# A hybrid decoder layer: stage seams, the top-k search's steps, and mixing's output projection in three passes

## The reference

```
hn = rms_norm(x, g_pre_mix);  q,k,v,index,deltanet,ssm parts = split(hn @ w_in)
o_a = attention over the 256 best keys of each query (index scores, top-k)
o_b = gated DeltaNet scan;  o_c = Mamba-2 scan            (causal convs + SiLU ahead)
mix = concat(o_a, o_b, o_c) @ w_out;   x = x + rms_norm(mix, g_post_mix)
hn = rms_norm(x, g_pre_x);  x = x + rms_norm(softmax((hn @ w_xq) mem_k) mem_v @ w_xo, g_post_x)
hn = rms_norm(x, g_pre_ffn); gate, up = hn @ w_gate, hn @ w_up
x = x + rms_norm((silu(conv3(gate)) * up) @ w_down, g_post_ffn)
```

## Time and profile before

| | us |
|---|---|
| median of 3 runs | 4142.58 (4139.6 to 4143.28) |
| the profiled execution | 4146.24 |
| its span, first to last instruction | 4144.1 |
| PE busy | 3807.1 (92%) |
| DVE, ACT, POOL busy | 1937.2, 1691.0, 654.3 |
| mean granted clock of PE | 0.943 |

### The profile page before, as it was taken

The page is one execution under the profiler, slowest core; times in us unless marked ns, Lnnn a source line. Parts: engine busy times, 40 slices in busy tenths (PEclk is TensorE's granted clock), DMA queues, the critical chain, the costliest instruction groups (busy, mean ns, idle before and its releaser), DMA issues. The chain is left out here.

```text
span 4144.1 us, 53976 instructions
## 1 busy us (share of the span) xinstructions
PE 3807.1 (92%) x20439; PEld 3243.0 (78%) x20439; DVE 1937.2 (47%) x3066; ACT 1691.0 (41%) x2923; POOL 654.3 (16%) x397
## 2 busy tenths in 40 slices
PE   8989999696888888699899996999999999799999
PEld 7879999443777777588655554999999999677777
DVE  3245551695888888698377544311211121321111
ACT  5531222594999999565332333111111111221111
POOL 0022121001444343000023001221112112000000
PEclk9999999776999999799999997999999999899999
DMA  3212124501111111410343321011111111332222
GB/s 117 91 51 75 71 97 160 142 8 43 40 37 35 49 35 34 128 51 27 128 133 117 113 82 55 22 63 42 42 63 42 42 57 48 127 115 80 86 76 65
DMA packets 200837, 299.17 MB, mean 72 GB/s; under 512 B 27804, under 2 KB 160596, under 8 KB 188220
## 3 DMA queue, kind: packets, MB, share of 16 engines
q1 hardware_dynamic: 198316, 296.69, 22.0%
q10 hardware_dynamic: 2336, 0.07, 0.0%
HBM read 193.96 MB, written 103.47 MB: 72 GB/s over the span
## 5 line engine op out<-in xcount | busy, mean ns | idle before, releaser
L1814 ACT ACTIVATE sn_junk<-sc_score,sl_nfb 128x640 bf16<-128x640 f32 (+12 forms) x416 | 577.0, 1389 | 1.5 <-DVE sl_nfb L1794 1.5
L3018 DVE TENSOR_SCALAR fu_acc<-fu_raw,fu_extra 128x2048 f32<-128x2048 f32 x22 | 28.3, 1286 | 741.6 <-ACT fu_up L2985 741.6
L156 PE MATMUL fu_p_g<-fu_hn_hi,fu_w_hi 128*128 128x412 f32 (+1 forms) x880 | 306.8, 349 | 20.4 <-POOL fu_w_lo L2972 20.4
L156 PE MATMUL fp_p_o<-fp_hn_hi,fp_w_hi 128*128 128x412 f32 (+1 forms) x840 | 295.0, 351 | 18.4 <-POOL fp_w_lo L498 18.4
L156 PE MATMUL fu_p_g<-fu_hn_hi,fu_w_lo 128*128 128x412 f32 (+1 forms) x880 | 309.0, 351 | 0.0
L156 PE MATMUL fu_p_u<-fu_hn_hi,fu_w_lo 128*128 128x412 f32 (+1 forms) x880 | 308.5, 351 | 0.0
L156 PE MATMUL fu_p_g<-all_hn_lo,fu_w_hi 128*128 128x412 f32 (+1 forms) x880 | 307.6, 350 | 0.0
L156 PE MATMUL fu_p_u<-all_hn_lo,fu_w_hi 128*128 128x412 f32 (+1 forms) x880 | 306.8, 349 | 0.0
L156 PE MATMUL fu_p_u<-fu_hn_hi,fu_w_hi 128*128 128x412 f32 (+1 forms) x880 | 306.0, 348 | 0.0
L3120 PE MATMUL fd_p_o<-fd_w_hi,fd_a_hi 128*128 128x512 f32 x680 | 272.7, 401 | 28.8 <-DVE fd_w_lo L3193 28.8
L156 PE MATMUL fp_p_o<-fp_hn_hi,fp_w_lo 128*128 128x412 f32 (+1 forms) x840 | 294.0, 350 | 0.0
(11 more groups left out here) (490 smaller groups left out, 8687.2 us busy)
## 6 DMA issues: line engine op xcount, KB each, us to landing
scratch_act<-fu_acc SPq DMA_DIRECT2D x22, 1088.0 KB, 4.9
fu_w<-in_w_gu SPq DMA_DIRECT2D x22, 1024.0 KB, 6.4
fd_a<-scratch_act SPq DMA_DIRECT2D x34, 640.0 KB, 4.6
scratch_conv<-fp_acc SPq DMA_DIRECT2D x14, 1028.0 KB, 3.9
scratch_halves<-fp_acc_lo SPq DMA_DIRECT2D x14, 1024.0 KB, 7.5
fp_w<-in_w_fm SPq DMA_DIRECT2D x21, 512.0 KB, 3.6
scratch_tm<-np_out SPq DMA_DIRECT2D x17, 524.0 KB, 2.7
np_x<-in_x SPq DMA_DIRECT2D x17, 512.0 KB, 3.9
```

Of the source, the lines that this page charges most:

```text
L156: last = pe.matmul(out, a, b, start=k == 0, stop=k == n - 1)
L1814: act.activation(self.junk[0:p, j % 2, 0:w], src, ACT.Sign, bias=self.nfb[0:p, n:n + 1].bitcast(F32), accum_out=self.cnt[0:p, n:n + 1]).th ...
L3018: dve.tensor_scalar(a, raw[:, 2:2 + SEQ], taps(i.t, 2), None, ALU.mult)
```

## The change

Seams: the first two weights of fp are loaded and split (POOL) at the end of np, whose last stores are waited for in fp; `masks` are loaded in fp, not in ix; `load_all` is gone, its loads are in the scan; waits for the scan's small constants come later. FFN down's first weight groups and activation tile are loaded at the end of fu into the room of `hn` (new class `DownFirst`). Search: the steps run one ahead (step 0 in pass -1, none of the second kind in the last pass), and `HERE` is 3: DVE counts one more block. Mixing: `w_out` and the mixing rows are split, `mixed` does three passes; `hn` goes tile by tile through one buffer `hnb` and device memory (`store_hn`), and fu loads it again, splitting its first weight on ACT and DVE. Page mask, recurrence and sample tiles move out of `hn`'s room.

```diff
+def split_weights(pool, N, i):
+    pool.wait_ge(N["c_w"][i.u], 16 * i.k + 16)
+    a, hi = N["w"][:, i.u], N["w_hi"][:, i.u]
+    pool.tensor_tensor(hi, a, N["one"][:].broadcast_to([P, D]), ALU.mult).then_inc(N["c_split"], 1)
+    pool.wait_ge(N["c_split"], 2 * i.t + 1)
+    pool.tensor_tensor(N["w_lo"][:, i.u], a, hi.bitcast(F32), ALU.subtract).then_inc(N["c_split"], 1)
@@ np, end: SP and POOL @@
+                for u in range(2):
+                    sp.dma_start(N["w"][:, u], A["w_fm"][u]).then_inc(N["c_w"][u], 16)
                 turns(sp, NT - 2, NT, store)
-                sp.wait_ge(c_store[0], 32 * ((NT + 1) // 2))
-                sp.wait_ge(c_store[1], 32 * (NT // 2))
+            @block.gpsimd
+                for u in range(2):
+                    split_weights(pool, N, Turn(0, u))
@@ fp, SP @@
-                turns(sp, 0, 2, load)
                 sp.dma_start(extra[:], A["extra"]).then_inc(c_extra, 16)
+                sp.dma_start(N["masks"][:], A["masks"]).then_inc(N["c_masks"], 16)
@@ scan, ACT @@
+                    one, two = 2 * t + 1, 2 * t + 2
+                    if t < 0:
+                        sel.count(act, two, HERE, SPLIT)
                     if here:
-                        sel.count(act, 2 * t, HERE, 6)
+                        sel.count(act, one, HERE, 6)
...
@@ scan, DVE @@
                         ssd_weigh(t)
+                        sel.count_here(dve, 2)
...
                         update_TT(t, 4)
+                    if nxt:
+                        sel.count_here(dve, 2)
...
-HERE, SPLIT = 2, 9
+HERE, SPLIT = 3, 9
@@ mixing, SP @@
+                def store_hn(t):
+                    vn.wait(sp, back(t), "hT2")
+                    sp.dma_start(A["hn"][tile(t)], hnb[:]).then_inc(c_hn, 16)
...
                     if ok(t + 3):
                         load_mix(t + 3)
...
+                    if t and t != AT + 1:
+                        store_hn(t - 1)
@@ mixing, ACT @@
+                def split_mix(t):
+                    act.wait_ge(c_mix[t % 2], 16 * (t // 2 + 1))
+                    act.activation(mix_hi[:, t % 2], mix[:, t % 2], ACT.Copy).then_inc(c_mhi, 1)
...
+                split_mix(0)
+                for n, part in enumerate(parts):
+                    act.wait_ge(c_wo[n], 16)
+                    act.activation(wo_hi[part], wo[part], ACT.Copy).then_inc(c_whi, 1)
+                split_mix(1)
                 norm_mix(0)
                 norm_x1(0)
+                split_mix(2)
...
                     if ok(t + 1):
                         norm_x1(t + 1)
+                    if ok(t + 3):
+                        split_mix(t + 3)
                     if 0 < t <= NB:
                         page_exp(t - 1)
@@ mixing, PE @@
-                        pe.wait_ge(c_mix[t % 2], 16 * (t // 2 + 1))
+                        pe.wait_ge(c_mlo, t + 1)
...
-                        last = pe.matmul(p_mix[:, c], mix[:, t % 2, k], wo[:, k, bass.ts(c, CHUNK)],
-                                         start=k == 0, stop=k == KT - 1)
+                        pe.matmul(p_mix[:, c], mix_hi[:, t % 2, k], wo_hi[:, k, n], start=k == 0, stop=False)
+                        pe.matmul(p_mix[:, c], mix_hi[:, t % 2, k], wo_lo[:, k, n], start=False, stop=False)
+                        last = pe.matmul(p_mix[:, c], mix_lo[:, t % 2, k], wo_hi[:, k, n], start=False, stop=k == KT - 1)
@@ mixing, POOL @@
+                pool.wait_ge(c_flip, 1)
                 pool.memset(K[:, NPG], 0.0)
@@ FFN up, SP @@
                 load(Turn(0, 0))
+                for t in range(NT):
+                    sp.dma_start(hn_all[:, :, bass.ts(t, P)], A["hn"][t]).then_inc(c_hn[chunk_of[t]], 16)
...
                 turns(sp, 4, FT, body)
+                sp.wait_ge(c_mm, 2 * NCH * FT)
+                sp.wait_ge(c_store, 16 * (FT - 2))
+                F.load_w(sp, A, 0)
+                F.load_a(sp, A, 0)
+                F.load_w(sp, A, 1)
+                F.load_w(sp, A, 2)
+                F.load_w(sp, A, 3)
                 store(Turn(FT // 2 - 1, 1))
@@ FFN up, ACT, in the loop over the five chunks (DVE's subtract stands likewise) @@
+                    if c == 0:
+                        act.wait_ge(c_w[0], 16)
+                        act.activation(w_hi[:, 0], w[:, 0], ACT.Copy).then_inc(c_split, 1)
@@ FFN up, POOL @@
-                turns(pool, 0, 2, body)
+                pool.wait_ge(c_lo, NCH)
+                turns(pool, 1, 2, body)
@@ FFN down's first loads @@
+    def load_w(self, sp, A, g):
+        lo, hi = self.GROUPS[g]
+        sp.dma_start(self.w[:, lo:hi], A["w_down"][:, lo:hi]).then_inc(self.c_w[g], 16)
+    def load_a(self, sp, A, j):
+        t, u = j // 2, j % 2
+        sp.dma_start(self.a[:, j % self.RING], A["act"][u * self.H:u * self.H + self.H, :, bass.ts(t, P)]
+                     .rearrange("f p n -> p f n")).then_inc(self.c_in[j % self.RING], 16)
```

More of the change, by code:

```diff
@@ L489, in _ @@
             def _(pool):
[L490 to L498, removed]
[L499 to L500 removed]
+                turns(pool, 2, FM, lambda i: split_weights(pool, N, i))
 G_IW, G_BETA, G_DT, G_G, G_A = 0, 8, 12, 20, 24
@@ L950, in _ @@
                     if here:
-                        sel.count(act, 2 * t, 6, SPLIT)
+                        sel.count(act, one, 6, SPLIT)
                     if nxt:
@@ L954, in _ @@
                     if here:
-                        sel.count(act, 2 * t, SPLIT, NSEL)
+                        sel.count(act, one, SPLIT, NSEL)
                     if prev:
@@ L959, in _ @@
                         ssd_decay(t)
-                        sel.count(act, 2 * t + 1, HERE, 6)
+                    if here and nxt:
+                        sel.count(act, two, HERE, 6)
                     if prev:
@@ L964, in _ @@
                         ssd_B(t)
-                        sel.count(act, 2 * t + 1, 6, 7)
-                        sel.count(act, 2 * t + 1, 7, SPLIT)
+                    if here and nxt:
+                        sel.count(act, two, 6, 7)
+                        sel.count(act, two, 7, SPLIT)
                     if nxt:
@@ L1204, in _ @@
                         update_TT(t, 3)
-                        sel.take(dve, 2 * t, 0)
-                        sel.propose(dve, 2 * t + 1, 0)
+                        sel.take(dve, one, 0)
+                    if here and nxt:
+                        sel.propose(dve, two, 0)
+                    if here:
                         masked(t, 4)
@@ L1212, in _ @@
                         sum_out(t - 1)
+                    if nxt:
+                        sel.count_here(dve, 1)
                     if here:
-                        sel.count_here(dve, 1)
                         update_T(t, 4)
-                        sel.take(dve, 2 * t, 1)
-                        sel.propose(dve, 2 * t + 1, 1)
+                        sel.take(dve, one, 1)
+                    if here and nxt:
+                        sel.propose(dve, two, 1)
                     if nxt:
@@ L2188, in stage_mix @@
         pt = s.sb("pt", [1, NB * NPG], I32)
-        row, cum, mb = (hn_all[0:NB, i, 0:W_S] for i in range(3))
+        row, cum = (K[0:NB].rearrange("b t c -> b (t c)")[:, i * W_S:i * W_S + W_S] for i in range(2))
+        mb = V[0:NB].rearrange("b t c -> b (t c)")[:, 0:W_S]
         par = s.sb("par", [NB, 2])
@@ L2916, in stage_ffn_up @@
         c_extra = s.sem("extra")
+        chunk_of = [max(c for c, (at, n) in enumerate(chunks) if at <= t * P) if t else 0 for t in range(NT)]
+        for c, (at, n) in enumerate(chunks):
+            chunk_of = [min(k, c) if t * P < at + n else k for t, k in enumerate(chunk_of)]
+        c_hn = s.sems("hn", NCH)
         with nc.Block() as block:
```

244 lines of the change are left out of this document (135 added, 109 removed).

## The result

| | before | after |
|---|---|---|
| median of four runs each, us | 4142.93 | 4191.28 (4181.15 to 4203.38) |
| the profiled execution, us | 4146.24 | 4181.15 |
| its span, us | 4144.1 | 4179.1 |
| PE busy, us | 3807.1 | 3771.6 |
| mean granted clock | 0.943 | 0.938 |

The ratio is 1.0112 [1.0093, 1.013]: +48.4 by the medians, where +22.5 was forecast. The two profiled executions are only 34.9 apart. The four runs after the change lie in two pairs (4181.15 and 4182.68; 4199.88 and 4203.38), so that the median stands between them, 10 above the profiled run; where the pairs come from is taken up further down.

A forecast was written before the change was run, and what follows sets the result against it. PE, busy for 92% of the span, was taken as the bound, but not in mixing's page loops. Terms summed to +22.5 us: 4168.7 by the profiled execution, 4165 by the median; range 4132 to 4195, the forecast's own 4150 to 4185.

The forecast's parts named there:

- np to fp: Seam into fp: no wait for stores, POOL's split moved into np; PE starts at 258.9, -9.5 us.
- fp to ix: Seam into ix: masks leave its queue, only their share of the loading, about 0.9 MB, goes; -3 us.
- ix to scan: Seam into the scan: a load stage and POOL's wait for small constants go; -4 us, bounds 0 and 9.
- scan: Search passes: a count moves from ACT to DVE, partly onto DVE's path; +4 us, bounds -26 and +28.
- mixing, start: Mixing before its first x2: page mask and mixing rows come later, first x2 at about 2108, not 2096.2; +12 us.
- mixing, page loops with the clock: Mixing's eight page loops: late mixing rows +21 us, PE's lower clock after its wait +21 us.
- mixing, other loops: Mixing from t = 9, without page loads: cheaper products save 3 a tile over seven tiles, -21 us.
- the held store: fu to fd: preloads hold back the last activation store; term -2 us, or -6 if the store weren't held.
- Rival 1: Mixing's page loops: the sum without the clock's loss, 4144; chance 0.16.
- Rival 2: Mixing's page loops: clock stays at half for the whole chain of each, 4190; chance 0.13.
- Rival 3: Scan: ACT sets the passes throughout, -26 instead of +4, not slower, 4135; chance 0.11.
- Rival 4: Mixing stays PE's, page loops 27.9 if rows landed by 10 after x2; not slower, 4091; chance 0.05.

The follow-up runs named there:

- the run of 4172.67: One run of the changed kernel measured once more, unchanged; the others there were 4181.9, 4182.3 and 4200.06, ratio 1.009.
- another start of mixing: On the changed kernel with the split behind the copy: page mask first, mixing's loads reordered; 4100.83 (4088.88 to 4124.65, six runs), ratio 0.9888.

## Why the prediction was right in direction and wrong in size

The direction and the mechanism in the page loops came as forecast. The step that failed is the sizing of mixing: its three terms, +12, +42 and -21, were to add up to +33, and they measured +55.3, 22 more. The scan's single figure, +4, failed too: the scan ran in two rhythms, -7.7 in the profiled run and +13.8 in the slower one, and the median of the changed kernel lies between the two.

Terms against the two profiled executions, in us:

| step | forecast | measured |
|---|---|---|
| np to fp | -9.5 | -9.7 (PE starts at 258.7; 258.9 forecast) |
| fp to ix | -3 | -0.9 (the seam 20.1 to 16.4, but PE's next waits there, for loads of keys and queries, 2.8 longer) |
| ix to scan | -4 | -7.5 (16.5 to 9.0) |
| scan | +4 | -7.7 (713.6 to 705.9); +13.8 in the slower rhythm |
| mixing, start | +12 | +16.8 |
| mixing, page loops with the clock | +42 | +51.2 (253.9 to 305.1) |
| mixing, other loops | -21 | -12.7 |
| mc to fu | +4 | +5.9 |
| fu to fd, and fd | -2 | -3.2 |
| fp, at with the seam ahead of it, fu | 0 | +2.6 |
| sum | +22.5 | +34.8 |

**Right: the mechanism of the page loops.** The split's wait stands ahead of `page_exp` and `copy_o`, the loop closes through SP's list, PE stands 4.4 and then runs at the lower clock; with the split put elsewhere the wait and the lower clock are both gone. In the loop shown the working gave 34.5 + 2.6 = 37.1; the trace has 37.4. Its parts: landing 16.8 after x2 (16.2 forecast; 5.7 after the issue instead of 4.7), page values 6.20 (4.07 and 2.6 for the clock: it was 2.1), from their end to `project` 4.1 (3.85), `project` 3.60, from its end to x2 5.4. The Trainium skill, "TensorE: Matmul & The Clock Gate", section "HAM oscillation — how this bites in real kernels", tells of a loop that waits for a DMA in each round and starts each round throttled. By that rule the page values run long in each round, and here the trace agrees: 6.20 against 4.07.

**Mis-sized: loop 8 and the landings, +9.** The seven other loops cost 41.4 in place of 36.8, most of it by the later landing. The DMA row of the loop shown, to be read beside the earlier trace rows:

```profile
mc_mix<-scratch_mixT SPq DMA_DIRECT2D x1, 512.0 KB, 5.7
```

In loop 8 the rows are asked for 16.0 after x2, not 11.2, behind the stores of the samples' states. It took 40.9, against 31.3 before, where I had counted eight equal loops:

```profile
2352.68 0.35 SPq L2317 DMA_DIRECT2D scratch_x<-mc_yo  x1
...
2362.58 1.13 SPq L594 DMA_DIRECT2D scratch_ys<-mc_ry  x2
...
2368.70 0.35 SPq L2250 DMA_DIRECT2D mc_mix<-scratch_mixT  x1
```

**Mis-sized: the start, +5.** Here "the pages are asked for some 2 later" failed. I read the mask's place on DVE, but not that the mask's new room holds back POOL's zeros and with them SP. In the changed kernel, stage start at 1997.3:

```profile
2027.27 0.75 DVE L1908 TENSOR_SCALAR mc_V<-mc_V 8x1152 f32<-8x1152 f32 x1
...
2029.26 0.31 POOL L2466 MEMSET mc_K<- 128x256 f32 x1 [379.26 <-PE mc_p_d L2862]
2030.91 8.08 SPq L2263 DMA_DIRECT2D mc_K<-in_k_pages  x8
...
2052.88 1.06 ACT L2365 ACTIVATE mc_mix_hi<-mc_mix 128x1024 fp32r<-128x1024 f32 x1 [20.46 <-DMA mc_mix<-scratch_mixT]
```

SP stands 15.2 for POOL's zeros there, where before it stood 13.9 for the page table, and the pages were asked for 33.6 after the stage's start, 4.4 later than before. Another 1.8 is the clock again, which I had counted in the page loops only: PE had waited for `copy_o(0)`, and `project(0)`, 3.60 in the sum, took 5.37 at a granted clock of 0.68.

```profile
2077.13 5.37 PE L2807 MATMUL mc_p_l<-wt_w_xo,mc_oT 128*128 128x512 f32 x8 [2.28 <-ACT mc_oT L2388]
```

**Mis-sized: the other loops, +8.** I had 3 off each; the plain ones went from 26.2 to 24.1. One plain loop before and one after (columns as above):

```profile
2432.50:2458.70 26.20, 26.20 (x122) 15.20 (x122) 12.52 (x13) 9.01 (x27) 0.00 (x0) 1.00 0.17 61
```

```profile
2459.30:2483.40 24.10, 23.53 (x137) 18.09 (x136) 13.60 (x15) 9.95 (x27) 0.00 (x0) 1.00 0.32 112
```

PE's busy time in a loop fell by 2.7, not by the 4 that I had counted (3.5 for the sets of three, the rest for the breaks between the pieces, for which I had no row). Next to that the chain costs little: PE waits 0.6 a loop for the next query's input.

**Wrong in sign: the scan, and one of its states unseen.** I took +0.9 a pass, the middle of my bounds, and the quick rhythm gives -0.3. What one trace couldn't show is that with the third block the scan falls into one of at least two rhythms. In the slower one, +13.8, my +4 was too small; three of the changed kernel's eight runs lie some 20 above the others. Of the 25.9 between +22.5 and +48.4 the stages of the profiled run hold 12.3; 10 is the place of the median between the two groups, and 3.3 the profiled run of the kernel before, that much above its median. That the upper group is the slower rhythm is shown for the profiled run of two other kernels only; for the runs without a profile it is inferred from their distance. What makes a run take one rhythm or the other was not found, and what the run of 4172.67 is stays open.

**Right: the held store.** fd waited 26.7, not 28.8 in two pieces. The last activation store landed late, as worked out from the earlier trace rows; the DMA row before and after:

```profile
scratch_act<-fu_acc SPq DMA_DIRECT2D x2, 1088.0 KB, 4.0
```

```profile
scratch_act<-fu_acc SPq DMA_DIRECT2D x1, 1088.0 KB, 8.6
```

Issued at 3630.68 behind 5.65 MB of preloads, it took 8.6 instead of 4.0; fd started at 3640.2. The Trainium skill, "DMA: Bandwidth & Descriptors", section "Queues, rings and completion order", says that descriptors are consumed in ring order. That spoke for the held store and a term of -2, and the trace agrees: 8.6, and a term of -3.2.

**The rivals.** Rival 1, no loss by the clock, is out (page values 6.20 instead of 4.07 at a granted clock of 0.67). Rival 2 came nearest by its time, 4190, for another reason: the clock was back within the chain of each loop. Rival 3, ACT setting all passes, is out too: the whole scan gained 7.7 in the quicker rhythm, not 26. Rival 4 (mixing stays PE's: 4091) is out for this kernel, and comes in part when the split is put out of the way: page loops of 30.8 in the middle, not 27.9, and 4114.57; only with another start of mixing as well did two runs, 4088.88 and 4090.17, go below its time.

## What to carry to other kernels

A new operation that waits for a DMA costs what stands behind it on its engine, so put it behind whatever others wait for; here that one place was worth 67 us, as much as the 68 that the cheaper products were to save at the most. When a tile's room is given a second use, follow every wait that the reuse adds, through each engine to the DMA queue, before saying what is late next. Where two engines of a loop are about level, look at more than one execution before pricing a shift of work between them: the loop may have two rhythms.

## What the runs showed of the hardware

- In a page loop in which PE waited 4.4 us its granted clock was 0.67 over the next 6.8 us, and the page values took 6.20 instead of 4.07; without the wait the whole loop ran at 1.00.
- The same scan code ran at 42.2 us a pass in one profiled execution and at 43.9 in another, with the half-clock stretches in some passes or, 7 us long, at one place in every pass from the second on; the runs of one kernel fell in two groups about as far apart. With one block of 640 columns more on ACT (0.81 us a step) the ten runs of two kernels lay in one group; so did the five runs of one kernel without it.
- A load of 512 KB that had landed 4.7 after its issue took 5.7 where a store of 512 KB is issued directly behind it; in loop 8, too, it took longer with the store behind it (4.4 instead of 3.6). Whether the store is the cause wasn't tried.
- A store of 1088 KB that landed 4.0 after its issue took 8.6 behind 5.65 MB of loads in the same queue.
